# Turns and compressed attention as one stage, and the index search in other places

## The reference

```python
topk = min(DSA_TOPK_MAX, S // 4)                      # S = 512
# first block, sparse attention with an index search, per block of 128 queries
rel = relu(einsum('bqhd,bkd->bqhk', q_idx, k_idx))         # 8 index heads of 32
score = einsum('bqh,bqhk->bqk', w_idx, rel)
score = where(key_pos <= qpos, score, -inf)
_, sel = lax.top_k(score, topk)
p = softmax(where(sel <= qpos, (q @ k[sel]) * scale, neg));  o = p @ v[sel]

# first block, retention, 4 heads, chunks of 128
inner = einsum('bnqhd,bnchd->bnhqc', qc, kc) * decay
out = einsum('bnhqc,bnche->bnqhe', inner, vc) + cross      # then a norm per head, silu gate

# second block, compression of keys and of values
def compress(kv, pe, w1, w2):                              # CMP_LEN 32, CMP_STRIDE 16
    n_cmp = (t - CMP_LEN) // CMP_STRIDE + 1                # 31
    idx = arange(n_cmp)[:, None] * CMP_STRIDE + arange(CMP_LEN)[None, :]
    blocks = kv[:, idx] + pe[None, None, :, None, :]
    blocks = blocks.transpose(0, 1, 3, 2, 4).reshape(b, n_cmp, g, CMP_LEN * d)
    return silu(blocks @ w1) @ w2                          # hidden width 128

kc, vc = compress(rope(k_cmp), ...), compress(v_cmp, ...)
s_c = einsum('bqgrd,bigd->bgrqi', qb, kc) * scale          # 6 heads, 2 groups of keys
p_c = masked_softmax(s_c, cmp_end <= tq)
o_c = einsum('bgrqi,bigd->bqgrd', p_c, vc)
out = g0 * o_c + g1 * o_selected + g2 * o_window
```

## Time and profile before

| what | us |
|---|---|
| median of three runs | 3441.42 |
| the three runs | 3436.34, 3441.42, 3455.11 |
| the profiled execution, whole | 3468.37 |
| its span in the trace | 3466.6 |

### The profile page before, as it was taken

The page is one execution under the profiler, slowest core; times in us unless marked ns, Lnnn a source line. Parts: engine busy times, 40 slices in busy tenths (PEclk is TensorE's granted clock), DMA queues, the critical chain, the costliest instruction groups (busy, mean ns, idle before and its releaser), DMA issues. The chain is left out here.

```text
span 3466.6 us, 48222 instructions
## 1 busy us (share of the span) xinstructions
PE 3234.7 (93%) x18592; PEld 2682.1 (77%) x18592; DVE 1899.0 (55%) x3628; ACT 1309.6 (38%) x2772; POOL 390.9 (11%) x368
## 2 busy tenths in 40 slices
PE   8999999999989999979899899999799989899996
PEld 6777788877767888768767878887688768788885
DVE  4775433436765424256475557474474765574754
ACT  4454332335354414243253333233442543332324
POOL 1021000010130000003002402010002024010010
PEclk9997999999999999989786999999898989999998
DMA  4110222222102222042000022332232000223321
GB/s 161 52 50 25 85 97 98 85 82 76 64 1 74 97 97 97 31 136 92 25 1 2 26 80 88 99 101 83 69 103 73 1 1 3 79 88 100 101 93 45
DMA packets 37341, 239.51 MB, mean 69 GB/s; under 512 B 4464, under 2 KB 5232, under 8 KB 15088
## 3 DMA queue, kind: packets, MB, share of 16 engines
q1 hardware_dynamic: 36528, 234.21, 19.9%
q10 hardware_dynamic: 576, 2.10, 0.2%
HBM read 234.19 MB, written 2.10 MB: 68 GB/s over the span
## 5 line engine op out<-in xcount | busy, mean ns | idle before, releaser
L260 PE MATMUL ps<-b_hl,bff_whl 128*128 128x512 f32 x704 | 275.7, 392 | 2.8 <-DVE b_hl L619 2.8
L261 PE MATMUL ps<-b_hl,bff_whl 128*128 128x512 f32 x704 | 275.1, 391 | 0.0
L262 PE MATMUL ps<-b_hl,bff_whl 128*128 128x512 f32 x704 | 274.9, 390 | 0.0
L243 DVE SCALAR_TENSOR_TENSOR bff_whl<-ring,b_cols,bff_whl 128x512 fp32r<-128x512 f32 (+1 forms) x224 | 153.2, 745 | 203.2 <-ACT bff_whl L230 203.0
L240 DVE TENSOR_TENSOR aff_whl<-ring,aff_whl 128x512 fp32r<-128x512 f32 x160 | 99.8, 686 | 223.7 <-ACT aff_whl L228 223.6
L230 ACT ACTIVATE bff_whl<-ring,b_cols 128x512 fp32r<-128x512 f32 (+1 forms) x224 | 136.6, 681 | 182.2 <-PE ps L262 182.2
L261 PE MATMUL ps<-aff_whl,a_u 128*128 128x512 f32 x512 | 204.3, 399 | 0.0
L260 PE MATMUL ps<-a_hl,aff_whl 128*128 128x512 f32 x512 | 200.9, 392 | 2.8 <-DVE a_hl L619 2.8
L260 PE MATMUL ps<-ain_whl,a_hl 128*128 128x512 f32 (+3 forms) x512 | 191.7, 374 | 11.1 <-DVE a_hl L619 7.2
L260 PE MATMUL ps<-aff_whl,a_u 128*128 128x512 f32 x512 | 201.7, 394 | 0.0
L262 PE MATMUL ps<-aff_whl,a_u 128*128 128x512 f32 x512 | 200.7, 392 | 0.0
(11 more groups left out here) (502 smaller groups left out, 7872.4 us busy)
## 6 DMA issues: line engine op xcount, KB each, us to landing
ring<-in_a_w_ff SPq DMA_DIRECT2D x64, 1024.0 KB, 4.7
ring<-in_b_w_up SPq DMA_DIRECT2D x32, 1024.0 KB, 4.9
ring<-in_a_w_in SPq DMA_DIRECT2D x16, 1024.0 KB, 5.8
ring<-in_b_w_down SPq DMA_DIRECT2D x16, 1024.0 KB, 4.8
ring<-in_b_w_in_att SPq DMA_DIRECT2D x12, 1024.0 KB, 4.9
ring<-in_b_w_up SPq DMA_DIRECT2D x16, 768.0 KB, 4.2
ring<-in_b_w_in_conv SPq DMA_DIRECT2D x12, 768.0 KB, 4.3
ring<-in_a_w_out SPq DMA_DIRECT2D x8, 1024.0 KB, 4.9
```

The costliest lines, as they stand in the source:

```text
L243: self.c.nc.vector.scalar_tensor_tensor(out=self.part(j, 1, k), in0=src[:, k, :], scalar=g[:, row + k:row + k + 1], in1=self.part(j, 0, k) ...
L260: nc.tensor.matmul(bank, sh, mh, start=start, stop=False)
L261: nc.tensor.matmul(bank, sh, ml, start=False, stop=False)
L262: return nc.tensor.matmul(bank, sl, mh, start=False, stop=stop)
```

## The change

**The search.** One round less stands ahead of the low parts of the ranks, and three rounds stand directly behind them. Those behind the chunks 14 and 15 stay. So 15 of the 16 rounds are in `projections_a`. The last round and the three multiplications no longer follow the retention's additions but are put singly between them (`late`), one after each addition from the third on.

**The merged stage.** `turned_and_compressed` takes the place of both stages. The 15 turns use four banks and are in another order: the compressed keys and values first (0 to 3), then the queries (4 to 6), the selected and window keys (7 to 10), the stick-breaking ones (11 to 14). The hidden products stand among the turns. `blocks` is gone: `kv2T` holds in its partitions 64 to 127 the same turned half shifted by one token, and a product reads its window directly, with a step of 16 words. Two more columns a group (`CMP_SEQ`) hold the position rows, so the product over 2 x 33 = 66 columns gives the contribution of the positions in its last column. ScalarE copies that into `bias` and adds it in the Silu. The addition of the mask to the scores is two instructions. The transposes of the probabilities alternate with the output products, head by head, on two banks each. GpSimd's four memsets form a chain.

```diff
-    def finish(self, dve, step, n):
-        self.steps = 0
-        for _ in range(n):
-            self.largest(dve, step)
-        for t in range(1, TT):
-            self.c.nc.vector.tensor_scalar(self.tile(t), self.tile(t), TAKEN, MASKED, ALU.not_equal, ALU.mult)
-
-
-SEARCH_EARLY = 13
+    def late(self, dve, step, i, rounds):
+        nc = self.c.nc
+        many = TT - 1
+        r, k = i // (2 * many), i % (2 * many)
+        t = 1 + k % many
+        if r < rounds and k < many:
+            step(nc.vector.max(self.best[:, t - 1, :], self.tile(t)))
+        elif r < rounds:
+            step(nc.vector.match_replace(self.tile(t), self.best[:, t - 1, :], self.tile(t), TAKEN))
+        elif r == rounds and k < many:
+            step(nc.vector.tensor_scalar(self.tile(t), self.tile(t), TAKEN, MASKED, ALU.not_equal, ALU.mult))
+
+
+SEARCH_EARLY = 15
...
-                    search.rounds(dve, (0, 0, 0, 2, 2, 1)[n])
+                    search.rounds(dve, (0, 0, 0, 2, 2, 0)[n])
...
                 for t in range(TT):
                     ranks.low(dve, t)
+                search.rounds(dve, 3)
                 dve.wait_ge(rooted, 2)
...
-                meanwhile(dve, step_sem)
+                        if h or j >= 2:
+                            beside(dve, step, TT * h + j - 2)
...
-                          lambda dve, step: search.finish(dve, step, TOPK // 8 - SEARCH_EARLY))
+                          lambda dve, step, i: search.late(dve, step, i, TOPK // 8 - SEARCH_EARLY))
...
-def compressed_attention(c, name, qT, blocks, pe_tiles, w2, gates, out, kcT, vcmp, kv2T):
+def turned_and_compressed(c, name, turns, pads, w2, pe_tiles, kv2T, qT, gates, out):
...
+    HID, SMALL = (4, 7), 4
+    score_at = lambda h: (5 + h % 2, h // 2 * TT * N)
...
+        windows = [kv2T[:, i].rearrange("p g (n r) -> p g n r", r=CMP_STRIDE) for i in range(2)]
+        hid_ps = [c.ps[:, HID[i], 0:G * NB].rearrange("p (g n) -> p g n", g=G) for i in range(2)]
...
+            def halves(i):
+                dst = turns[i][1]
+                if isinstance(dst, tuple):
+                    late = SEQ - dst[1].shape[-1]
+                    return [(dst[0], c.ps[0:HD, i % 4, 0:SEQ]), (dst[1], c.ps[HD:P, i % 4, late:SEQ])]
+                return [(dst, c.ps[:, i % 4, :])]
...
-                for i in range(2):
+                def turn(i):
+                    src = turns[i][0]
+                    if i >= 4:
+                        wait_kept(pe, i - 4)
+                    for t in range(TT):
+                        part, twice = src(t)
+                        dst = c.ps[:, i % 4, t * P:(t + 1) * P]
+                        if twice:
+                            for r in (0, HD):
+                                ins = nc.tensor.matmul(dst[r:r + HD], part, c.ident, start=True, stop=True)
+                        else:
+                            ins = nc.tensor.transpose(dst, part, c.ident)
+                    ins.then_inc(turned, 1)
+
+                def hidden(i):
                     c.wait_chunk(pe, first + i)
                     wt = c.chunk(first + i)
-                    pe.wait_ge(summed, i + 1)
+                    pe.wait_ge(pe_here, 1)
+                    wait_kept(pe, 2 * i)
+                    wait_kept(pe, 2 * i + 1)
                     for m in range(CMP_LEN // 2):
-                        ins = nc.tensor.matmul(c.ps[:, i, 0:G * N], wt[:, m, :], blocks[:, i, m, :],
+                        o, r = m // 8, 2 * (m % 8)
+                        ins = nc.tensor.matmul(hid_ps[i], wt[:, m, :], windows[i][:, :, o:o + NB, r],
                                                start=(m == 0), stop=(m == CMP_LEN // 2 - 1))
                     ins.then_inc(c.chunk_used, 1)
+                for i in range(7):
+                    turn(i)
+                hidden(0)
+                turn(7)
+                turn(8)
+                hidden(1)
+                turn(9)
+                turn(10)
...
+                for i in range(12, len(turns)):
+                    turn(i)
                 pe.wait_ge(masked, 1)
-                for h in range(H):
-                    for t in range(TT):
-                        ins = nc.tensor.transpose(c.ps[0:N, h, t * P:(t + 1) * P], s[:, h, t, :], c.ident)
-                    ins.then_inc(turned, 1)
-                for h in range(H):
-                    pe.wait_ge(turned_kept, h + 1)
-                    for t in range(TT):
-                        ins = nc.tensor.matmul(c.ps[:, h, t * HD:(t + 1) * HD], pT[:, h, t * P:(t + 1) * P],
-                                               vcmp[0:N, h // NSA_R, :], start=True, stop=True)
-                    ins.then_inc(outs, 1)
+                for h in range(H + 1):
+                    if h < H:
+                        if h >= 2:
+                            pe.wait_ge(p_kept, h - 1)
+                        for t in range(TT):
+                            ins = nc.tensor.transpose(c.ps[0:N, 5 + h % 2, t * P:(t + 1) * P], s[:, h, t, :], c.ident)
+                        ins.then_inc(p_turned, 1)
+                    g = h - 1
+                    if g >= 0:
+                        pe.wait_ge(p_kept, g + 1)
+                        pe.wait_ge(small_kept, 2)
+                        if g >= 2:
+                            pe.wait_ge(outs_kept, g - 1)
+                        for t in range(TT):
+                            ins = nc.tensor.matmul(c.ps[:, HID[g % 2], t * HD:(t + 1) * HD], pT[:, g, t * P:(t + 1) * P],
+                                                   vcmp[0:N, g // NSA_R, :], start=True, stop=True)
+                        ins.then_inc(outs, 1)
...
-                    nc.scalar.activation(hid[:, i, :], c.ps[:, i, 0:G * N], ACT.Silu).then_inc(silus, 1)
+                    nc.scalar.copy(bias[:, i:i + 1], hid_ps[i][:, 0, NB - 1:NB]).then_inc(biased, 1)
+                    act.wait_ge(biased, i + 1)
+                    nc.scalar.activation(hid[:, i, :].rearrange("p (g n) -> p g n", g=G), hid_ps[i][:, :, 0:N], ACT.Silu,
+                                         bias=bias[:, i:i + 1]).then_inc(silus, 1)
+
+                for i in (0, 2, 4, 6):
+                    keep(i)
...
-                    for gr in range(G):
-                        by16 = kv2T[:, i, gr, :].rearrange("p (i r) -> p r i", r=16)
-                        for b in range(2):
-                            r = slice(b * HD, (b + 1) * HD)
-                            for o in range(2):
-                                ins = nc.vector.tensor_tensor(
-                                    blocks[r, i, 8 * o:8 * o + 8, gr * N:(gr + 1) * N],
-                                    by16[r, b:16:2, o:o + N],
-                                    pe_tiles[r, 16 * i + 8 * o:16 * i + 8 * o + 8].unsqueeze(2
-                                             ).broadcast_to([HD, 8, N]), ALU.add)
-                    ins.then_inc(summed, 1)
+                    for g in range(G):
+                        ins = nc.vector.tensor_copy(kv2T[:, i, g, SEQ:].rearrange("p (m b) -> p m b", b=2)[:, :, 0],
+                                                    pe_tiles[:, 16 * i:16 * (i + 1)])
+                ins.then_inc(pe_here, 1)
+                for i in (1, 3, 5, 7, 9):
+                    keep(i)
                 dve.wait_ge(small, 1)
...
-                step(nc.vector.tensor_tensor(flat, c.ps[:, 0:H, 0:TT * N],
-                                             neg.unsqueeze(1).broadcast_to([P, H, TT * N]), ALU.add))
+                for b in range(2):
+                    ins = nc.vector.tensor_tensor(
+                        flat[:, b::2], c.ps[:, 5 + b, 0:H // 2 * TT * N].rearrange("p (h n) -> p h n", h=H // 2),
+                        neg.unsqueeze(1).broadcast_to([P, H // 2, TT * N]), ALU.add)
+                step(ins)
                 step(nc.vector.tensor_reduce(st[:], s[:], AX.X, ALU.max))
...
-            kv2T = sb1("kv2T", [P, 2, NSA_G, SEQ])
-            transpose_tiles(c, "nsaT", jobs, clear)
...
-                blocks = sb2("blocks", [P, 2, CMP_LEN // 2, NSA_G * N_CMP])
-                compressed_attention(c, "cmp", qT, blocks, cols["pe"], cols["w2"], gates, out4, kcT[:], vcmp, kv2T)
+                kv2T = ctx2.enter_context(nc.sbuf_tensor("b_kv2T", [P, 2, NSA_G, CMP_SEQ], F32))
...
+                turns = [(twice(a + g * HD), (kv2T[0:HD, i, g, 0:SEQ], kv2T[HD:P, i, g, 0:SEQ - 1]), 1.0)
+                         for i, a in ((0, B_KC), (1, B_VC)) for g in range(NSA_G)]
...
+                turned_and_compressed(c, "cmp", turns, pads, cols["w2"], cols["pe"], kv2T, qT, gates, out4)
```

102 lines of the change are left out of this document (69 added, 33 removed).

## The result

The changed kernel took 3419.72 us (median of 20 runs, 3406.91 to 3445.42), the kernel before 3456.09 us in 20 runs beside them (3425.72 to 3483.94; the three shown above are the first of these). The ratio is 0.992, with a 95% interval from 0.9895 to 0.9945. The ratios in this document leave out runs over 1.5% above the fastest of their kernel, and they are not quotients of medians. The quotient of the two medians would be 0.9895 (36.4 us), at the lower end of the interval. Set against the 3441.42 us from which the prediction started, the ratio gives 27.5 us less, 19 to 36 with the interval. The forecast was 38 less. The direction was right. The median of 3419.72 lies between the outer ends of the forecast, 3380 and 3428, but above its main range of 3390 to 3416; the ratio applied to 3441.42 gives 3414. The gain by the ratio is 0.72 of the forecast one (0.5 to 0.95 by the interval).

A forecast was written before the change was run, and what follows sets the result against it. TensorE, busy 93% of the span, was taken as the bound, so edits pay where it waits or runs slowly. 27.2 + 8.0 + 2.3 = 37.5, say 38, off 3441.4 gives 3403 us; own range 3390 to 3416, outer ends 3380 and 3428.

The forecast's parts named there:

- merged stage, a layer: Turns and compressed attention as one stage: 42.5 us a layer against 56.1, 27.2 us won in both layers.
- projections, two layers: First block, search round ahead of the ranks' low parts removed: 4.0 us a layer won, 8.0 for both.
- second layer's retention: Last search round spread over the retention: 2.3 us won at the upper level, nothing in the first layer.
- The hidden products: Merged stage, 64 records over 66 columns: 0.122 us each, 7.8 us, the strided read taken to cost nothing.
- The gap: Merged stage, TensorE's wait ahead of the first probability transposes: about 3.8 us, with the lower level expected behind it.
- VectorE's chain to chunk 16: Projections: VectorE's work from 154.43 ends at 183.0, where TensorE's products on chunk 16 had started at 187.21.
- the alternation: End of merged stage, four transposes alternating with products: 15.3 us without a clock rise, where the old form took 12.7.
- To the transposes: Merged stage, from scores to probability transposes: scores 3.2 us, then 5.3 us to the masked probabilities.
- The clock did not hold to the end of the stage: First rival: clock holds through the merged stage, last part 8.8 us instead of 15.3, 13 us more won, 3390; chance 0.10.
- the hidden products did not slow: Second rival: strided read slows them and the clock falls there; only about 10 us stay, 3431; chance 0.16.
- The top price of 298 ns a record: Third rival, slower: hidden products' strided read at 298 ns a record, 10.4 us extra over 128 records; chance 0.03.
- Rival 4: Second layer's retention loses the clock: 8.4 us plus about 3 more, the 2.3 not won, 3417; chance 0.13.

The follow-up runs named there:

- before: The kernel without the change, in its first profile (profiled execution 3468.4 us); 3456.09 us in 20 runs beside the changed kernel.
- before_again: The kernel before, unchanged, run once more for a second profile: one execution of 3436.1 us, old stages 53.2 and 53.1 us.
- search_only: The kernel before with the search's part of the change alone; ratio to the kernel before 0.9984 (0.9957 to 1.001).
- merge_only: The changed kernel with the index search put back as before; ratio to the kernel before 0.9911 (0.9884 to 0.9937).
- rows_first: The changed kernel with the 24 probability transposes in a row again ahead of the output products; ratio to the kernel before 0.9841 (0.9811 to 0.9871).
- filled_gap: The changed kernel with 30 more identity transposes behind turn 14, where TensorE waits; ratio to the kernel before 0.9897 (0.9859 to 0.9935).
- exp_early: The changed kernel with a small Exp on ScalarE behind the second Silu, loading the table early; one execution, 8.29 and 8.28 us to the transposes.
- turns_in_gap: The changed kernel with transposes in a row, early Exp table, six turns behind the scores, copies dealt anew; ratio to the kernel before 0.9827 (0.9775 to 0.9879).
- round_behind: turns_in_gap with the last search round and its three multiplications behind the retention's additions again; ratio to the kernel before 0.9866 (0.9818 to 0.9913).
- side_by_side: The changed kernel with hidden products reading 66 adjacent columns, not stepped by 16 words; one execution, 12.17 against 12.43 us from first product to scores.

## Why the prediction was off in size

The sum of the prediction, beside what the profiles showed (old form: `before`, `before_again` and `search_only`; new: the changed kernel twice and `merge_only`; both layers of each):

| term | predicted | measured |
|---|---|---|
| old pair of stages, a layer | 56.1 | 56.1, 56.1, 53.2, 53.1, 56.1, 53.0: mean 54.6 |
| merged stage, a layer | 42.5 | 45.2, 44.0, 44.9, 44.0, 44.0, 44.0: mean 44.3 |
| gain of it, two layers | 27.2 | 20.5 |
| projections, two layers | 8.0 | 8.4 (4.1 and 4.3) |
| second layer's retention | 2.3 | 2.3 at the upper level, none at the lower |
| sum | 37.5 | 31 at most, 27.5 in the runs (19 to 36) |

**What held.** The hidden products: 64 records in 7.74 us, predicted 7.8, at a granted clock of 1.00. That was the point I called most doubtful. The sum has prices of the upper level up to the scores, and the clock was 1.00 from the stage's start to their end. Their 48 records took 3.44 us, where the sum has half of 6.31. From the stage's start to them 5.01, predicted 5.1. The gap, 3.79 us, predicted 3.8. The wait for the low parts, 0.40. VectorE's chain to chunk 16: it began at 153.27 in place of 154.43, and TensorE's products started at 181.95, which is 183.1 with those 1.16 added; predicted 183.0. Waits of 1.17 (new) and 0.25 (from 0.91 to 1.16) stand where 1.8 was predicted. The retention of the second layer, 22.77 against 25.03.

**The first step that failed: the alternation, priced at nothing in the last part.** I put 15.3 us for transposes and output products, and 0.8 behind them. It took 17.85, in each of six layers. I had the level right (0.50 to the end of the stage), and the price of a record inside its group too: the sum's 0.217 is 13.89/64 of L3070, at a granted clock of 0.50 from 1672.9 to 1687. By the timeline above eight transposes take 1.91 and four 1.06, sixteen output records 3.67 and eight 1.97, so one record more costs 0.2125 us, and 72 x 0.2125 = 15.3. What my sum had at nothing is the change from one kind to the other. Four transposes take 0.99 and eight output records 1.90 from start to start, 2.89 a head, where twelve records at 0.2125 are 2.55. The changes are most of the 1.75 us by which the last part was longer than forecast, 3.5 in both layers. Why a change costs time the runs don't tell. `rows_first` shows that the alternation was a loss of the change: the old order takes 13.5 in the same place. By the working above I estimate that about a third of those 4.3 us is the changes, and the rest the clock, which rises behind the row of transposes (0.50, then 1.00).

**The second: one profile as the measure of the old form.** I compared with 56.1 us. Three of six layers took 53.0 to 53.2, because the clock held after the row of transposes (1.00 in all three; 5.57 us for the 48 output records, where it is 8.20 in the earlier trace rows). On average I began 1.5 us a layer too high, 3 in all. The profiled execution lay 27 us above the median, and I said so, but I subtracted the gain as if it were the same in both. The start of the forecast was low as well: the three runs had a median of 3441.42, all twenty 3456.09. Those 14.7 us are most of the 16.7 by which the measured median lies above 3403, and they say nothing of the change.

**Smaller.** To the transposes I put 3.2 + 5.3 = 8.5. It was 8.69 where turns 12 to 14 ran fast (1.53 us) and up to 9.86 where not (2.70). I had these turns at nothing, but the last one's copy on ScalarE leads to the table load, to Exp and so to the transposes. I also hadn't asked whether the clock holds behind the scores; in the first layer it was at 0.53 there.

**The rivals.** The clock did not hold to the end of the stage (0.50), the hidden products did not slow (0.12 us a record), and nothing was slower than before. The top price of 298 ns a record took each column as read twice. That was an estimate, and no run shows a second read. In the trace of the kernel before, two plain fp32 records take 0.44 us over 128 columns and 1.08 over 512 (225 to 231), so 0.83 ns a column for each, and the records of a split product stand 0.23 us apart over 512 (188 to 192), 0.45 ns a column: 1.9 times. Rival 4, the second layer's retention at the lower level, did not happen in the two profiles of the changed kernel (22.77 and 22.78 us), but it did in four of the six others with the spread round. A retention takes 36.4 to 37.3 us at the lower level against 22.8 or 25.0, in either layer and with either form. I gave it 0.13 for one layer; over 24 layers of the twelve profiles it happened in 11. It is a spread on both sides of the change, and for one execution it is half as large as the whole effect.

**What stays open.** Two spreads, in the retentions and in the delta net behind the merged stage, are as large as the effect or half of it, and in these profiles they pull in different directions. The retentions of the spread form fell to the lower level in 10 of 16 layers, the others in 1 of 8. The first layer's delta net took 148.7 to 156.1 us in the three profiles with the old stages and 131.9 to 138.1 in seven of the nine with a merged one (149.1 and 155.0 in the others, `filled_gap` and `exp_early`), while in the second layer it was 134.9 to 138.4 with the old stages and about 141 in most of the others (151.0 in `turns_in_gap`, 133.7 in `round_behind`). Twelve profiles can't tell whether the change shifts these odds or they fell so. The sum of 31 and the runs' 27.5 agree only in so far as these two cancel or are chance.

## What to carry to other kernels

Where a stage's time depends on a clock that rises and falls inside it, take the old time from more than one execution, since the profile on hand shows one draw (53.0 to 56.1 us for the same old stage). Moving work under a wait paid twice here, since it closed the gap (33 us in place of 44 with the same work, the transposes of the probabilities at a granted clock of 1.00 in place of 0.50), while interleaving two kinds of small products cost time twice, at each change of kind and in a clock that never rose from 0.50: 17.85 against 13.5. Spreading a serial chain over another engine's waits gained nothing once the chain was short enough to end before the stage's last engine (at 990.77, with the next stage at 995.26).

## What was not expected of the hardware

TensorE's clock went down to the lower level behind 6.8 us in which the engine was busy for 6.57, and stayed there while it was busy for 10.07 of 10.50 (`filled_gap`, 0.50 at 1689.5 to 1700). It did output products over 31 rows and small transposes in turn. In `rows_first` the clock came back at the end of a row of 24 transposes (0.50, then 1.00). At the lower level a head of twelve records with its changes of kind took 2.89 us, where twelve times the price of one more record (0.2125) is 2.55. A read of 66 columns with a step of 16 words cost 4 ns a record on TensorE (12.43 us against 12.17 with the 64 records, `side_by_side`). VectorE's additions with such a step took 561 ns for 248 elements against 424 for 256, but those two instructions differ in more than the step, and no run separates it.
